# Retention outputs in a 1-core two-block model kernel: from plain float32 products to three products of rounded high and low parts

## The reference, cut to what matters

```python
proj = rmsnorm_2(h, g_norm) @ w_in
q, k, v, gate = jnp.split(proj, [RET_QK_W, 2 * RET_QK_W, 2 * RET_QK_W + RET_V_W], axis=-1)
...
s = jnp.einsum('bhnd,bhmd->bhnm', qc, kc) * decay
o = (jnp.einsum('bhnm,bhmv->bhnv', s, vc)
     + jnp.einsum('bhnd,bhdv->bhnv', qc, state) * q_dec[..., None])
...
o = ((o - mu) * lax.rsqrt(var + EPS)).transpose(0, 2, 1, 3).reshape(b, t, RET_V_W)
o = o * gn_gain.astype(jnp.float32)
y = (jax.nn.silu(gate.astype(jnp.float32)) * o).astype(h.dtype) @ w_out
```

## Time and profile before

| | |
|---|---|
| median of 3 runs | 1186.5 us (1186.36 to 1186.7) |
| the profiled execution's own time | 1186.84 us |
| its span, first to last instruction | 1185.1 us |
| mean granted TensorE clock | 0.997 |
| PE busy | 1159.4 us, 98% |
| PE weight loads | 1010.1 us, 85% |
| DVE busy | 871.8 us, 74% |
| ACT busy | 626.6 us, 53% |
| chain of work that ended last | PE 90%, DVE 6%, ACT 2%, issue 2% |

### The profile page before, as it was taken

One profiled execution on the slowest core, in us unless ns is written; L12 is line 12 of the kernel. 1 busy time (PEld: TensorE's weight loads), 2 busy tenths in 40 slices (PEclk: granted clock), 3 DMA queues, 4 the chain that ended last, 5 costly groups with the idle time before them and its releaser, 6 DMA issues.

```text
span 1185.1 us, 18031 instructions
## 1 busy us (share of the span) xinstructions
PE 1159.4 (98%) x7262; PEld 1010.1 (85%) x7262; DVE 871.8 (74%) x1437; ACT 626.6 (53%) x979; POOL 15.3 (1%) x33
## 2 busy tenths in 40 slices
PE   6999999999999999999999999999999999999996
PEld 6968888888899878888889978878798899999885
DVE  5876699998867768999989766665676257777654
ACT  6635555665654455665565334434552356666552
POOL 0000000000000000000000000000010000000000
PEclk9999999999999999999999999999999999999998
DMA  9944545555443324556555544454576523332351
GB/s 382 316 125 164 181 165 198 202 186 202 170 171 138 112 86 171 178 206 213 178 178 178 185 151 184 165 178 142 213 279 255 213 98 107 108 111 104 128 190 39
DMA packets 33027, 205.87 MB, mean 174 GB/s; under 512 B 4400, under 2 KB 5040, under 8 KB 10416
## 3 DMA queue, kind: packets, MB, share of 16 engines
q1 hardware_dynamic: 32944, 204.71, 49.0%
HBM read 200.72 MB, written 1.05 MB: 170 GB/s over the span
## 4 chain that ended last, share of the span: by engine, by line
PE 90%; DVE 6%; ACT 2%; issue 2%; DMA 0%; DVEq 0%; POOLq 0%; POOL 0%; SPq 0%; ACTq 0%
PE bank L804 20%; PE bank L805 19%; PE bank L806 19%; PE bank L810 12%; PE bank L811 6%; PE bank L966 2%; DVE WL L1724 2%; PE bank L1232 1%; PE bank L1314 1%; ACT WH L1340 1%; PE bank L1206 1%; PE bank L1295 1%; PE bank L949 1%; PE bank L1030 1%; PE bank L1003 1%
## 5 line engine op out<-in xcount | busy, mean ns | idle before, releaser
L1724 DVE TENSOR_TENSOR WL<-RAW,WH 128x2048 fp32r<-128x2048 f32 x172 | 393.3, 2289 | 119.2 <-ACT WH L1340 117.1
L1340 ACT ACTIVATE WH<-RAW 128x2048 fp32r<-128x2048 f32 x172 | 328.0, 1910 | 169.9 <-PE bank L806 169.3
L810 PE MATMUL bank<-X,WH 128*128 128x512 f32 x704 | 250.4, 399 | 2.0 <-DVE work L1798 1.7
L811 PE MATMUL bank<-X,WL 128*128 128x256 f32 x704 | 197.6, 281 | 0.0
L804 PE MATMUL bank<-WH,MH 128*128 128x512 f32 (+1 forms) x480 | 181.5, 378 | 0.0
L806 PE MATMUL bank<-WH,ML 128*128 128x512 f32 (+1 forms) x480 | 178.7, 372 | 0.0
L805 PE MATMUL bank<-WL,MH 128*128 128x512 f32 (+1 forms) x480 | 178.6, 372 | 0.0
L804 PE MATMUL bank<-X,WH 128*128 128x256 f32 x560 | 162.1, 289 | 11.1 <-DVE WL L1958 10.8
L810 PEld LDWEIGHTS bank<-X,WH 128*128 128x128 f32 x704 | 132.2, 188 | 36.5 <-DVE work L1798 2.8
L805 PE MATMUL bank<-X,WH 128*128 128x256 f32 x560 | 159.3, 284 | 0.0
L806 PE MATMUL bank<-X,WL 128*128 128x256 f32 x560 | 159.1, 284 | 0.0
(11 more groups left out here) (287 smaller groups left out, 1689.7 us busy)
## 6 DMA issues: line engine op xcount, KB each, us to landing
RAW<-wstream SPq DMA_DIRECT2D x173, 1024.0 KB, 4.9
con<-cmpw SPq DMA_DIRECT2D x6, 512.0 KB, 5.5
xn<-cmpw SPq DMA_DIRECT2D x4, 512.0 KB, 7.0
con<-consts SPq DMA_DIRECT2D x1, 1617.0 KB, 6.6
con<-tapw SPq DMA_DIRECT2D x3, 512.0 KB, 7.6
X<-work SPq DMA_DIRECT2D x16, 71.5 KB, 3.3
work<-xT_in SPq DMA_DIRECT2D x1, 1024.0 KB, 5.1
x<-x_in SPq DMA_DIRECT2D x1, 1024.0 KB, 8.1
```

Source lines behind the costliest of these rows:

```text
L810: mm(o[:, 0:2 * T], w[0], X2[:, k, :, :].rearrange("p a t -> p (a t)"), start=start, stop=False)
L811: return mm(o[:, T:2 * T], w[1], XH[:, k, :], start=False, stop=stop)
L1340: act_fn(WH[:, t % RING, :], RAW[:, t % RING, :], ACT.Copy).then_inc(w_rounded, 1)
L1724: tt(WL[:, t % RING, :], RAW[:, t % RING, :], WH[:, t % RING, :].bitcast(F32), ALU.subtract).then_inc(w_split, 1)
```

## The change

The decayed scores and the values are each split into a rounded high part and a low remainder, and the outputs are made with `three`:

- ACT writes the values' high part `rvh` (rounded) where it wrote `rv`; it no longer frees the bank. Then it waits until DVE has the decayed scores in `sdt`, and rounds them into `sdh`.
- DVE, after the multiplication by the decay table, waits until this has ended and drains, then writes the values' low part `rvl` out of PSUM, one instruction of 128 x 512 for each chunk, and these free the values' banks. Then it writes `sdl`, the scores' low part (128 x 384).
- PE waits for `sdl` and runs nine float32r matmuls for each head in place of three plain float32 ones.
- The parts lie in halves of existing buffers: PH and PL for the scores, the last four slots of MH and ML for the values. `sdt` has one buffer in place of two.

```diff
@@ -226,7 +226,7 @@
         gemm(("rk", h), "dve")
     for h in range(RH):
         for i in range(TT):
-            gemm(("rv", h, i, "out"), "act", ("rv", h, 1))
+            gemm(("rv", h, i, "out"), "dve", ("rv", h, 1))
         aux("B", ("rs", h), "dve")
         if h:
             for j in range(2):
@@ -461,8 +461,9 @@
-        sdt = wk(5120, 2, 384)
-        rv = wk(5888, TT, 512)
+        sdt = wk(5120, 384)
+        sdh, sdl = (w[:, :, :].rearrange("p a t -> p (a t)")[:, 0:384] for w in (PH, PL))
+        rvh, rvl = (w[:, 12:16, :].rearrange("p (i b) t -> p i (b t)", i=TT) for w in (MH, ML))
@@ -564,6 +565,10 @@
+        decayed = sem("decayed")
+        decay_rounded = sem("decay_rounded")
+        decay_split = sem("decay_split")
+        rv_rounded = sem("rv_rounded")
@@ -1197,13 +1202,13 @@
                 gemm_n(("rg", h), XH, XL)
-                is_free(pe, ("rs", h))
+                pe.wait_ge(decay_split, h + 1)
                 is_free(pe, ("rv", h, 1, "out"))
                 for i in range(TT):
                     o = take(("ro", h, i))
                     for m in range(i + 1):
                         a = m * T + (i - m) * P
-                        last = mm(o[:, :], sdt[:, h % 2, a:a + P], rv[:, m, :], start=(m == 0), stop=(m == i))
+                        last = three(o[:, :], 512, (sdh[:, a:a + P], sdl[:, a:a + P]), (rvh[:, m, :], rvl[:, m, :]), m == 0, m == i)
                     last.then_inc(aux_done, 1)
@@ -1611,8 +1616,9 @@
                 for i in range(TT):
                     ready(act, ("rv", h, i, "out"))
-                    free(act_fn(rv[:, i, :], B(("rv", h, i, "out"))[:, :], ACT.Copy, scale=rstd[:, 6, i:i + 1]),
-                         ("rv", h, i, "out"), "act")
+                    act_fn(rvh[:, i, :], B(("rv", h, i, "out"))[:, :], ACT.Copy, scale=rstd[:, 6, i:i + 1]).then_inc(rv_rounded, 1)
+                act.wait_ge(decayed, h + 1)
+                act_fn(sdh, sdt, ACT.Copy).then_inc(decay_rounded, 1)
                 if h:
                     ret_out(h - 1)
@@ -2163,7 +2169,15 @@
                 ready(dve, ("rs", h))
-                free(tt(sdt[:, h % 2, :], B(("rs", h))[:, 0:384], const("decay")[:, h * 384:(h + 1) * 384], ALU.mult), ("rs", h), "dve")
+                free(tt(sdt, B(("rs", h))[:, 0:384], const("decay")[:, h * 384:(h + 1) * 384], ALU.mult), ("rs", h), "dve")
+                is_free(dve, ("rs", h))
+                dve.drain().then_inc(decayed, 1)
+                for i in range(TT):
+                    dve.wait_ge(rv_rounded, TT * h + i + 1)
+                    free(stt(rvl[:, i, :], B(("rv", h, i, "out"))[:, :], rstd[:, 6, i:i + 1], rvh[:, i, :].bitcast(F32),
+                             ALU.mult, ALU.subtract), ("rv", h, i, "out"), "dve")
+                dve.wait_ge(decay_rounded, h + 1)
+                tt(sdl, sdt, sdh.bitcast(F32), ALU.subtract).then_inc(decay_split, 1)
                 if h:
                     ret_low(h - 1)
```

## The result

| | before | after |
|---|---|---|
| median | 1186.53 us (15 runs, 1185.67 to 1191.34; all but one at most 1187.18) | 1189.1 us (15 runs, 1188.7 to 1189.75) |
| ratio after to before | | 1.0021, 95% interval 1.0014 to 1.0028 |
| profiled execution's own time | 1186.84 | 1189.6 |
| its span | 1185.1 | 1187.8 |

The changed kernel is slower by 0.21%, 2.6 us. The forecast was 1189.1. It is slower beyond doubt, since the interval lies above 1; whether by more than 0.2% the interval leaves open.

The account below looks back on a forecast made before the run. The prediction took PE, busy 98% of the span, as the bound. Stalls of 4.8 us less a 2.15 us product gain made +2.65, written as +2.6 on 1186.5: 1189.1 us, range 1187.8 to 1190.3.

Parts of the forecast that it names:

- The products: Outputs of each head: nine float32r matmuls at 0.227 us replace three plain ones, gaining 0.54 us per head.
- Rival 2: Outputs' products: each float32r product costs 0.215 us, a fourth of a plain one; +2.2 us, 1188.7; chance 8%.
- The drain: On DVE between decay multiplication and values' low part: wait and drain cost 0.14 us, bounds 0.03 and 0.20.
- The low parts: On DVE, freeing the values' banks: two 128x512 instructions reading PSUM take 1.41 us, bounds 1.28 and 1.53.
- The stall: PE waits 1.60 us at the gate's first weight load in heads 1 to 3, none in head 0; 4.8 together.
- Rival 1: Gate's first weight load, heads 1 to 3: bank free in time, not slower, 1184.3 us without stall; chance 6%.
- rival 3: Gate's banks: a shorter stall of 1.0 to 1.3 us, +0.8 to +1.7, 1187.3 to 1188.2; chance 14%.
- The cover: Scores' low part has over 8 us of room before the outputs, the next tile's split 6 us; no cost.
- rival 4: DVE becomes the bound, late tile splits or low parts costing each head 0.5 to 1 us more, +4 to +6; chance 10%.
- The clock: PE's clock stays at 2.4 GHz, since no stall is longer than 1.8 us and PE works gaplessly around each.
- The chances: Whole kernel: slower by over 0.2% 60%, within 0.2% 37%, faster by over 0.2% 3%.
- PE's busy time: In the profile after, PE busy was to fall by about the sum of gain and stalls.

Follow-up runs that it names:

- e2: The changed kernel with the turned head (ry) in ring B, so the gate no longer takes the same head's values' banks; 1184.36 us.
- e8: e2 with a fourth product, low by low, for each output, three matmuls more per head; 1187.6 us.
- e5: The changed kernel without DVE's wait and drain between decay multiplication and values' low parts; ACT waits for the freed scores' bank instead; 1188.43 us.
- e3: The kernel before, with plain products, in which DVE also writes an unread low part of the values and so frees their banks; 1191.35 us.
- e6: e2 with the order of e4 on DVE, the scores' low part ahead of the values' low parts; 1184.25 us.
- e4: The changed kernel with DVE writing the scores' low part ahead of the values' low parts; 1194.73 us.
- e1: The changed kernel with DVE's two low parts of the values ahead of the decay multiplication; 1185.83 us.

## Why the prediction was right

- **The products.** Predicted 0.54 us of gain per head from 11 steps of 0.227; measured 0.55 in head 0, 0.56 in e2's others. Rival 2, with 0.215 for each product and a gain of 0.65, is out: the nine starts in the changed kernel are 0.227 apart, and three more matmuls in e8 took 0.68.
- **The drain.** Predicted 0.14 us between the multiplication and the low part; it is 0.15 (712.69 to 712.84). e5 shows that it is on the path, and that the overlap of two instructions goes with it.
- **The low parts.** Predicted 1.41 us for two, from a row with the scalar operand and none with these operands; measured 1.41, 0.746 each. By the rule that the prediction cites from the Trainium skill (VectorE: DVE Perf Modes, The DRAIN you can't avoid), no overlap, it would have been 2 x 0.746 = 1.49. The same section adds that a next instruction that is not held starts earlier, which the prediction left out; these rows agree with that, the second starting 0.67 behind the first.
- **The stall.** Predicted 1.60 us in heads 1 to 3 and none in head 0; the weight loads waited 1.58 three times, released by the line that was named. Rival 1 (no stall) and rival 3 (1.0 to 1.3 us) are out by that. e3 has it without the rest of the change.
- **The cover.** The scores' low part ends at 714.71, far ahead of the outputs. The turned low part starts 1.2 us later behind the scores than before and the next tile split 0.6 us; neither shows on PE, and e2 and e6 show that this work is free. With no wait ahead of the outputs or of a tile, rival 4 is out.
- **The clock.** Predicted to stay at 2.4 GHz, and it did: 1.00 in the stage. But the reason given, that no stall is longer than 1.8 us, was thinner than it sounded. e4 shows it lost behind stalls only 1 us longer. No rival had a price for such a loss, which e4 puts at 1.6 us for each fall.
- **The chances.** 60% lay on slower by over 0.2% and 37% within; the measured 0.21% is on the line between the two, and the interval holds both.
- **Luck.** The terms hold to some hundredths of a microsecond in the profile, and that isn't luck. That the median meets the forecast's 1189.1 to the tenth is: the interval of the ratio reaches from 1.7 to 3.3 us.
- **What it had wrong.** PE's busy time was to fall by about the sum of gain and stalls, which is some 7 us; it fell by 1.4. A stall adds idle time, it takes no busy time away: PE's matmuls waited 4.1 us more in a span that is 2.7 us longer, and 2.7 - 4.1 = -1.4. Nothing in the forecast's sum rests on that sentence.

## What to carry to other kernels

When an instruction that frees a buffer is moved to another engine, or one that reads it is added, ask who takes that buffer next and when, and what stands ahead of the new reader on its own engine. Averages don't tell: DVE was idle a third of the stage, and the two instructions fitted in easily, only not in the 0.66 us in which PE needed them. Before shortening such a path look at the plan of buffers: one word in the bank plan (e2) gave back the whole stall, which a better order on DVE (e1, e5) only shortened.

## What was not expected of the hardware

The clock fell behind stalls of 2.6 us (e4), in two of three heads, to 0.50 for 3.4 us, beginning 1.0 and 1.4 us after PE had taken up work again, and some eight matmuls ran at 0.43 us in place of 0.227, 1.6 us each time. Behind stalls of 1.3 to 1.6 us in the profiles of the changed kernel, e3 and e5 it stayed at 1.00. So a stall's price need not be its length: at 2.6 us it came to 4.2. What decides between the two, and why head 1 was spared, wasn't tried and stays open.
